# A two-model transformer kernel on one core: norm chains interleaved, retention moved forward, modulation rows turned four at a time

## The chip, the cores and the metric

The kernel runs on one core of one Trainium2 chip. The metric is the device time of one execution in microseconds (us). "PE" is TensorE, "DVE" VectorE, "ACT" ScalarE, "POOL" GpSimd, "SP" SyncE; "ACTq" in a row is a DMA issued by ScalarE. Matrices are float32 (precision is kept by splitting, see below); weights stream in from HBM, activations stay in SBUF.

## The reference, cut to what matters

```python
# first_block: DEPTH = 2, 256 latent and 256 context tokens, width 1024
for i in range(DEPTH):
    ml = split(silu(c) @ w_ada[i] + b_ada[i], 6)       # modulation, 2 streams
    mc = split(silu(c_ctx) @ w_ada[i] + b_ada[i], 6)
    u = modulate(h, g_pre_mix[i], ml[0], ml[1])        # rms_norm(h)*(1+scale)+shift
    o = even_mixer(u) if i % 2 == 0 else odd_mixer(u)  # recurrence + window | 2 attentions
    h = h + ml[2] * rms_norm(o @ w_out[i], g_post_mix[i])
    f = sqrelu_mlp(modulate(h, g_pre_ff[i], ml[3], ml[4]), w_ff1[i], w_ff2[i])
    h = h + ml[5] * rms_norm(f, g_post_ff[i])
# second block: 256 tokens, on the latent stream
p = rms_norm_2(h) @ w_in_2     # nsa q, k, v, gates | retention q, k, v, gate | 2 x 1024 gates
nsa = nsa_attention(...)       # compressed, selected and window attention
ret = retention(q, k, v)       # 4 heads; normed, times silu(gate)
z = sigmoid(ga[:, :1024]) * (nsa @ w_nsa_branch) + sigmoid(ga[:, 1024:]) * (ret @ w_ret_branch)
h = h + z @ w_mix_out; u = rms_norm_2(h); out = h + gated_mlp(u)  # with a short convolution
```

## The kernel before, in words

The whole computation is one static program. A Python function writes a **plan**, a list of steps; each engine runs through the plan and issues its own part of every step, so the order of the plan is the order of each engine's queue. Nothing is scheduled at run time: an engine blocks at its next instruction until the semaphores that it names have come.

**Weights** come in chunks of 128 x 2048 through a ring of four SBUF slots loaded by SyncE. A projection is done with split numbers: ScalarE rounds a chunk into one of three `HIGH` buffers (`split`, L2473), VectorE subtracts to leave the low part (L1906), and PE multiplies high x high, high x low and low x high in three matmuls (L1412, L1413, L1414). `early` is the place in the plan at which the next chunk's split is put: one chunk ahead. The modulation slices are not split (`whole`).

**Modulation**: 24 slices of `w_ada` per layer, two layers. `mod(i, s)` is 16 small matmuls of 128x256 (L1463) into a PSUM bank, four row groups of 32; ScalarE copies the rows (L2473, 128x256), and `turn` transposes and sums them with 4 instructions on PE (L1470) and one add on VectorE (L1899). Eight slices stand at the very front, eight in the even stage (45 to 249 us), 32 as filler in the recurrence (249 to 640 us).

**Norm chains.** Four stages end in a row projection with `gate`: mix0, ff0 (its chain is `m1`), mix1, ff1 (`m2`). For a token block of 128, "out block" takes the sum from PSUM (L1972), ScalarE squares it (L2551), VectorE gates it (L1975); `normed` then does: residual (L1961, 128x1024), square and root on ScalarE (L2514, L2516), inverse (L1931) and scale rows (VectorE L1936, half 0; ScalarE L2520, half 4), transposes on PE (L1477), out of PSUM with the modulation (VectorE L1948, ScalarE L2538), x hi (ScalarE, L2473 128x512), x lo (VectorE, L1955 128x512, two of them). mix0 and ff0 have four token blocks, mix1 and ff1 two. The next stage's projection waits for x lo. The first steps of ff1 are cut into halves of two tokens (`ff1 half`).

**Odd attention** begins with `odd start` (ScalarE issues five DMAs of tables) and qD, kD, vD. The **second block** begins with `second start` (eleven such DMAs) and qN, a projection over both token blocks. There `run(n_prepare(), r_proj())` takes the two generators in turn: the attention of the second block, and retention's q, k, its values vr, gates gr and the merge gates ga. When both have ended, `merge start` takes the sigmoid of ga (L2794, 128x4096) and the silu of gr (L2796), and the four retention heads (`ret s` L1822, `ret o` L1830, scores from PSUM L2370) run beside the projection of the nsa branch. `ret norm`, `ret gated` (L2400) and `ret turn` (PE L1844, L2407) follow alone, and then the ret branch.

## Time and profile before

| | us |
|---|---|
| median of 3 runs | 2057.84 |
| lowest, highest | 2055.41, 2064.58 |
| the profiled execution | 2063.38 |
| its span in the trace | 2061.6 |
| PE busy | 1844.8 |
| DVE busy | 1100.0 |
| ACT busy | 904.6 |
| POOL busy | 216.2 |

Busy time is from the trace. Matmuls overlap, so a group's sum can be more than the time that it fills. An idle time in brackets is that of the engine right before the row's first instruction, with what ended it.

### The profile page before, as it was taken

What the parts mean: (1) busy time and instruction counts of PE and PEld (TensorE: products, weight loads), DVE (VectorE), ACT (ScalarE), POOL (GpSimd) and SP (SyncE); (2) the same over time, 40 slices, a digit from 0 to 9 for tenths busy, and PEclk for the clock granted to TensorE, in tenths of its full rate; (3) what the DMA queues carried; (4) which work ended last, traced back from release to release, by engine and by line L of the source; (5) the groups of instructions that cost most, each with busy time, mean ns of one, the idle gap of its engine ahead of it and who ended that gap; (6) DMA issues with size and microseconds to landing.
All of it is one profiled execution on the core that took longest, in us unless ns stands there. A gap on an engine that the chain in (4) does not pass through costs nothing.

```text
span 2061.6 us, 39782 instructions
## 1 busy us (share of the span) xinstructions
PE 1844.8 (89%) x16802; PEld 1537.0 (75%) x16802; DVE 1100.0 (53%) x1671; ACT 904.6 (44%) x1448; POOL 216.2 (10%) x214
## 2 busy tenths in 40 slices
PE   5899879899888889999996999799979999679997
PEld 3777658778777778888886776698877677569985
DVE  1457565465555554324435766565445674556863
ACT  3326545344332353223325356565342465346652
POOL 0000034425253000000000200010000000000210
PEclk9999889999998989999998999899989999789998
DMA  8332233222231222333233420355544434245543
GB/s 272 94 123 90 91 112 105 85 84 84 84 105 64 82 82 82 102 102 93 91 102 72 124 81 28 107 182 187 192 131 155 152 103 139 72 132 164 184 156 110
DMA packets 201375, 237.16 MB, mean 115 GB/s; under 512 B 14347, under 2 KB 158573, under 8 KB 201197
## 3 DMA queue, kind: packets, MB, share of 16 engines
q1 hardware_dynamic: 195856, 227.33, 34.7%
q10 hardware_dynamic: 5341, 7.30, 1.0%
q8 instruction: 132, 2.16, 0.4%
q14 instruction: 46, 0.38, 0.1%
HBM read 233.56 MB, written 1.05 MB: 114 GB/s over the span
## 4 chain that ended last, share of the span: by engine, by line
PE 75%; DVE 11%; ACT 7%; issue 2%; POOL 2%; DMA 1%; SPq 1%; ACTq 1%; DVEq 0%; POOLq 0%
PE bank L1412 18%; PE bank L1413 17%; PE bank L1414 17%; PE bank L1604 9%; ACT window L2473 2%; DVE window L1906 2%; PE bank L1592 2%; PE bank L1571 2%; PE bank L1583 2%; PE bank L1463 1%; PE bank L1611 1%; SPq L2934 1%; PE bank L1789 1%; ACT arena L2538 1%; PE bank L1575 1%
## 5 line engine op out<-in xcount | busy, mean ns | idle before, releaser
L1412 PE MATMUL bank<-window 128*128 128x512 f32 (+1 forms) x2152 | 768.6, 357 | 64.8 <-DVE window L1955 27.8
L1413 PE MATMUL bank<-window 128*128 128x512 f32 (+1 forms) x2152 | 754.1, 350 | 0.0
L1414 PE MATMUL bank<-window 128*128 128x512 f32 (+1 forms) x2152 | 753.8, 350 | 0.0
L1412 PEld LDWEIGHTS bank<-window 128*128 128x128 f32 x2152 | 419.6, 195 | 131.1 <-DVE window L1906 32.4
L1906 DVE TENSOR_TENSOR window<-arena,window 128x2048 fp32r<-128x2048 f32 (+1 forms) x164 | 371.4, 2265 | 272.3 <-ACT window L2473 270.4
L2473 ACT ACTIVATE window<-arena 128x2048 fp32r<-128x2048 f32 (+3 forms) x292 | 377.1, 1291 | 198.3 <-PE bank L1414 121.4
L1414 PEld LDWEIGHTS bank<-window 128*128 128x128 f32 x2152 | 419.0, 195 | 50.9
L1413 PEld LDWEIGHTS bank<-window 128*128 128x128 f32 x2152 | 420.2, 195 | 48.1 <-issue 0.2
L2473 ACT ACTIVATE arena<-bank 128x256 f32<-128x256 f32 (+1 forms) x298 | 127.0, 426 | 370.7 <-PE bank L1414 134.9
L1604 PE MATMUL bank<-arena 64*64 64x64 f32 (+1 forms) x5888 | 218.1, 230 | 18.9 <-DVE arena L1398 10.5
L1604 PEld LDWEIGHTS bank<-arena 64*64 64x64 f32 x5888 | 204.8, 139 | 35.4 <-DVE arena L1398 12.2
L2880 POOL TENSOR_TENSOR arena<-arena 128x256 f32<-128x256 f32 x80 | 67.8, 848 | 409.1 <-ACT arena L2473 303.1
L2695 ACT ACTIVATE arena<-bank 128x512 f32<-128x512 f32 (+1 forms) x64 | 31.4, 491 | 142.0 <-PE bank L1414 140.7
L2108 DVE TENSOR_TENSOR arena<-arena,bank 128x512 f32<-128x512 f32 (+1 forms) x80 | 50.7, 634 | 64.7 <-PE bank L1604 63.7
L2597 ACT ACTIVATE arena<-bank,arena 128x512 f32<-128x512 f32 (+3 forms) x112 | 58.5, 522 | 55.0 <-DVE arena L2052 34.0
L2241 DVE TENSOR_TENSOR arena<-arena 128x512 f32<-128x512 f32 (+1 forms) x48 | 29.0, 603 | 78.8 <-ACT arena L2695 78.3
L1463 PE MATMUL bank<-arena 128*32 128x256 f32 x768 | 58.3, 426 | 13.3 <-DMA arena<-in_w_ada 13.1
L2052 DVE TENSOR_REDUCE arena<-bank 128x1 f32<-128x512 f32 (+4 forms) x96 | 51.7, 538 | 22.9 <-PE bank L1575 17.0
L2902 POOL TENSOR_TENSOR arena<-arena 128x2048 f32<-128x2048 f32 x2 | 11.1, 5560 | 483.1 <-DMA arena<-in_c_rpb 483.1
L2473 ACT ACTIVATE extra<-bank 128x512 f32<-128x512 f32 (+2 forms) x96 | 46.9, 489 | 19.4 <-PE bank L1583 16.8
L1470 PEld LDWEIGHTS bank<-arena 128*128 128x128 f32 x192 | 29.0, 213 | 25.5 <-ACT arena L2473 12.1
L1477 PE MATMUL bank<-arena 128*128 128x128 f32 x144 | 26.2, 347 | 23.8 <-DVE arena L1936 23.3
(286 smaller groups left out, 1668.1 us busy)
## 6 DMA issues: line engine op xcount, KB each, us to landing
arena<-in_w_ff SPq DMA_DIRECT2D x64, 1024.0 KB, 5.3
arena<-in_w_ada SPq DMA_DIRECT2D x48, 1024.0 KB, 5.7
arena<-in_w_in SPq DMA_DIRECT2D x23, 1024.0 KB, 5.1
arena<-in_w_ffn_up SPq DMA_DIRECT2D x22, 1024.0 KB, 5.1
arena<-in_w_ffn_down SPq DMA_DIRECT2D x10, 1024.0 KB, 5.1
arena<-in_w_in_even SPq DMA_DIRECT2D x9, 1024.0 KB, 5.5
arena<-in_w_out SPq DMA_DIRECT2D x8, 1024.0 KB, 5.1
arena<-in_w_in_odd SPq DMA_DIRECT2D x8, 1024.0 KB, 5.3
```

The costliest lines, as they stand in the source:

```text
L1412: e.matmul(o, rr(l[0]), rr(r[0]), start=start, stop=False)
L1413: e.matmul(o, rr(l[0]), rr(r[1]), start=False, stop=False)
L1414: return e.matmul(o, rr(l[1]), rr(r[0]), start=False, stop=stop)
L1463: t = e.matmul(u.b[q:q + 32, 0:256], SV[:, k, :], w.v[:, k, :], start=k < 4, stop=k >= 4)
L1571: t = e.matmul(b if it["ns"] > 1 else b[:, 0], it["q"][h0:h1], k, start=True, stop=not it["masks"])
L1604: t = e.matmul(o[h0:h1, c], l[i][h0:h1, c], r[i][h0:h1, c], start=i == 0, stop=i == len(l) - 1)
L1906: e.tensor_tensor(rr(raw), raw, rr(w.high, F32), SUB).then_inc(*ve.tick(w.ready))
L2052: e.tensor_reduce(low[:, h * ns:h * ns + ns], b, AX.X, MAX, negate=True).then_inc(*ve.tick(at("max", S, i, h)))
L2108: e.tensor_tensor(w, w, x, SUB).then_inc(*ve.tick(b.empty, at("w", *u)))
L2473: return e.activation(o, i, ACT.Copy, **k)
L2597: e.activation(a.P[i % a.NP][h][:, s * n:s * n + n], u.b[:, s * n:s * n + n], ACT.Exp, bias=low[:, x:x + 1], accum_out=total[:, x:x + 1]). ...
L2880: return e.tensor_tensor(z.L[l % 2], z.G[:, :, 0], lvl[:, 1 - d, l:l + 1, :].to_broadcast([128, NCH, 64]), MUL)
```

## The change

1. **Shared turns.** Four slices of the modulation accumulate in one PSUM bank: slice g of four shifts the two input columns by 2g rows (`SV` is 38 wide, `sel` 8). One copy of rows and one `turn` follow for each four. The bank is held over four slices.
2. **Norm chains.** The chains of token blocks are taken up at other places between the matmuls of the last out blocks; `out gate` is a step of its own; the last two chains end together (`ends`) between the first matmuls of the next stage. Scale rows is done by VectorE in both halves; x lo of half 4 is GpSimd's. `early` can hold two places: the second chunk of the next stage is split right behind the first token block's steps, its low part by GpSimd (128x2048), its high part in a fourth `HIGH` buffer, lent by `extra` outside the attentions. `ff1 half` and qD wait for both halves of two tokens' x lo.
3. **Constants.** `odd start` and `second start` come behind vD and behind the kv projections.
4. **Values first.** In the second block the first half of vr stands ahead of qN; it is a row projection of one token block at a time, and waits for that block alone.
5. **Retention.** Its heads, norm, gating and turning are a part of the first generator now and run beside the last projections of ga and the nsa branch; silu of gr comes first, the sigmoid in two halves (`gates 0`, `gates 1`). Each of the retention steps waits for what it reads. `oT` lies in H and GB.

```diff
+    turns = [0, 1, 2]
+    early = []
     chunks = {}
+    def lend(name):
+        high_free[3] = tuple(stage(name))
+        turns.insert(1, 3)
+    def back():
+        turns.remove(3)
     class Chunk:
...
+                n, w.pool = early.pop(0)
+                plan.insert(n, ("split", key))
+                early[:] = [(n + 1, q) for n, q in early]
+        if not early or whole and len(early) == 1:
+            here()
     def here():
-        early[0] = len(plan)
+        early[:] = [(len(plan), False)]
     def cols(key, W, c0, n, k0=0, nk=8, whole=False):
...
-    order_of_mod = []
+    order_of_turn = []
     def mod(i, s):
         cols(("mod", i, s), I["w_ada"][i], s * 256, 256, whole=True)
-        take("mod", i, s)
-        order_of_mod.append((i, s))
...
-        give("mod", i, s)
-    def turn_row(i, s):
-        take("turn", i, s)
-        step("turn", i, s)
-        give("turn", i, s)
+        if s % 4 == 3:
+            order_of_turn.append((i, s // 4))
+            step("rows", i, s // 4)
+            give("mod", i, s // 4)
+    def turn_rows(i, g):
+        take("turn", i, g)
+        step("turn", i, g)
...
     def modulation(i, f0=0, f1=24):
-        prev = None
         for s in range(f0, f1):
...
-                turn_row(i, prev)
-            prev = s
-            yield
-        turn_row(i, prev)
+            if s % 4 == 0 and s > f0:
+                turn_rows(i, s // 4 - 1)
+            yield
+        turn_rows(i, f1 // 4 - 1)
...
                 elif y == len(parts) - 1:
                     for m in range(ntok):
                         step("out", name, c, y - 1, (m,))
-                        if then and m > 1:
-                            next(then[m - 2])
+                        last, before = [then[i:i + 1] if i >= 0 else () for i in (m - 1, m - 2)]
+                        on_by(before, 1)
+                        on_by(last, 1)
+                        on_by(before, 2)
                         step("out", name, c, y, (m,))
-                        if then and m > 1:
-                            next(then[m - 2])
-                            next(then[m - 2])
                         step("out block", name, c, m)
+                        on_by(last, 1)
+                        if gate:
+                            step("out gate", name, c, m)
                         give("out", name, c, m)
-                        if then:
-                            last = then[m - 1] if m == ntok - 1 else iter(())
-                            next(last, None)
-                            for _ in range(3):
-                                next(then[m])
-                                next(last, None)
+                        on_by(then[m:m + 1], 1)
+                        if then and not m:
+                            early.append((len(plan), True))
             if c == 0:
                 for m in range(ntok):
                     step("out block", name, c, m)
+                    if gate:
+                        step("out gate", name, c, m)
                     give("out", name, c, m)
-        trailing[:] = then[-1:]
-        if ntok == 2:
-            trail()
+        trailing[:] = [ends(*then[-2:])] if then else []
+    def on_by(gens, n):
+        for g in gens:
+            for _ in range(n):
+                next(g)
+    def ends(a, b):
+        on_by([a, b, a, a, b], 1)
+        yield
+        on_by([b], 1)
+        yield
+        on_by([b], 2)
+        yield
     def trail(n=3):
...
+                if j == 0 and n == 256:
+                    trail()
...
                     for f in range(4):
                         take("ff1", i, 0, f)
-                    step("ff1 half", i, 0, (0, 1, 2))
+                    step("ff1 half", i, 0, (0,))
+                    trail(1)
+                    step("ff1 half", i, 0, (1, 2))
                     trail(1)
...
-            trail(2 * j - 3)
+        trail((1, 0, 1, 1)[j])
     cols(("kD",), W_o, 2048, 128)
     take("kD")
     step("kD")
...
     qN, KCV, KSW = sb(4, 256), sb(2, 2, 256), sb(2, 2, 256)
-    step("second start")
     second_x = xr
+    def values_gates(nm, j, c0, between):
+        for k in range(2):
+            take(nm, j, k)
+        for y in range(2):
+            cols((nm, j, y), W_2, c0 + j * 512, 512, y * 4, 4)
+        for k in range(2):
+            for y in range(2):
+                step("vg", nm, j, y, k)
+                if not k:
+                    between()
+            give(nm, j, k)
+    trail(1)
+    values_gates("vr", 0, 2328, lambda: trail(1))
+    trail()
     for j in range(4):
         if j % 2 == 0:
             cols(("qN", j // 2), W_2, j * 128, 256)
             take("kv", nm, g)
             step("kv", nm, g)
...
+    def retained():
+        step("end", "second attention")
+        attended.append(True)
+        step("ret start")
+        step("gates", 0)
+        spreads["ret",] = (lambda k: col("ret_gn_w_2", k), gwr, stage("second attention"))
+        yield from spread_(("ret",))
+        step("ret gates")
+        yield from staggered_(retention(h) for h in range(4))
+        step("ret norm")
+        step("gates", 1)
+        yield
+        for i in range(2):
+            step("ret gated", i)
+            yield
+            for q in (0, 4):
+                take("ret turned", i, q)
+                step("ret turn", i, q)
+                give("ret turned", i, q)
+                yield
+    def n_then_ret():
+        yield from n_prepare()
+        while len(r_turned) < 8:
+            yield
+        yield from retained()
...
-    spreads["ret",] = (lambda k: col("ret_gn_w_2", k), gwr, stage("second attention"))
-    run(spread_(("ret",)))
-    step("ret gates")
-    run(branch("nsa", I["w_nsa_branch_2"][0], 4), staggered_(retention(h) for h in range(4)))
...
+    def r_then_branch():
+        for n, _ in enumerate(r_proj()):
+            yield
+            if attended or n > 24 and n % 2:
+                yield
+        while not attended:
+            yield
+        for _ in branch("nsa", I["w_nsa_branch_2"][0], 4):
+            yield
+            yield
+    back()
+    r_turned, attended = [], []
+    run(n_then_ret(), r_then_branch())
+    step("end", "retention")
+    lend("retention")
...
+            w, u, g = chunks["mod", i, s], bank("mod", i, s // 4), s % 4
             pe.wait_ge(w.landed, u.before, at("sv"))
             for k in range(8):
                 q = 32 * (k % 4)
-                t = e.matmul(u.b[q:q + 32, 0:256], SV[:, k, :], w.v[:, k, :], start=k < 4, stop=k >= 4)
-            t.then_inc(*pe.tick(u.full, w.used))
...
-            e.tensor_scalar(scaled_rows(k, 0), rows_of(k, 0), RS[:, k, 2:3], None, MUL).then_inc(*ve.tick(at("scaled rows", T, k, 0)))
+            for q in (0, 4):
+                e.tensor_scalar(scaled_rows(k, q), rows_of(k, q), RS[:, k, 2:3], None, MUL).then_inc(*ve.tick(at("scaled rows", T, k, q)))
         def norm_x(T, k, q):
...
+        def ret_start():
             sc.wait_ge(sc.last(), *stage("second attention"))
             load(landed_decay, at("decay"), [(dec, C["dec"])])
             copy(rr(oNh), oN).then_inc(*sc.tick(at("oN rounded")))
-            sc.wait_ge(sc.last())
-            e.activation(ga, ga, ACT.Sigmoid).then_inc(*sc.tick(at("gates")))
-            sc.wait_ge(sc.last())
+            sc.wait_ge(sc.last(), *[at("vg", "gr", j, 1) for j in range(2)])
             e.activation(gr, gr, ACT.Silu).then_inc(*sc.tick(at("gr")))
+        def gates(i):
+            g = ga[:, :, 1024 * i:1024 * i + 1024]
+            sc.wait_ge(sc.last(), *[at("vg", "ga", 2 * i + j, 1) for j in range(2)])
+            e.activation(g, g, ACT.Sigmoid).then_inc(*sc.tick(at("gates", i)))
...
+        def split(key):
+            w = chunks[key]
+            if w.pool:
+                raw = w.ap[:, 0:w.n]
+                gp.wait_ge(gp.last(), w.rounded)
+                e.tensor_tensor(rr(raw), raw, rr(w.high, F32), SUB).then_inc(*gp.tick(w.ready))
         def part_o(k):
...
```

VectorE at the end of ff0, third and fourth token block, before (L1961 residual, L1936 scale rows, L1948 out of PSUM, L1955 x lo, L1972 and L1975 the last out block):

```order
L1975 TENSOR_TENSOR arena<-arena 128x512 [waits scalar_done,vector_done]
L1931 RECIPROCAL arena<-arena 128x1 [waits scalar_done,vector_done]
L1961 SCALAR_TENSOR_TENSOR arena<-arena 128x1024 [waits vector_done]
L1931 RECIPROCAL arena<-arena 128x1 [waits scalar_done,vector_done]
L1936 TENSOR_SCALAR arena<-arena 128x4x128 [waits vector_done]
L1948 TENSOR_SCALAR arena<-bank,arena 128x128 [waits tensor_done,vector_done]
L1948 TENSOR_SCALAR arena<-bank,arena 128x128 [waits vector_done] x3
L1955 TENSOR_TENSOR window<-arena,window 128x4x128 [waits scalar_done,vector_done] x2
L1969 TENSOR_SCALAR arena<-arena 128x1 [waits vector_done]
L1972 TENSOR_TENSOR arena<-arena,bank 128x512 [waits tensor_done,vector_done]
L1975 TENSOR_TENSOR arena<-arena 128x512 [waits scalar_done,vector_done]
L1948 TENSOR_SCALAR arena<-bank,arena 128x128 [waits tensor_done,vector_done]
```

The same stretch with the change (L2052 residual, L2026 scale rows, L2038 out of PSUM, L2046 x lo, L2063 and L2072 the out block):

```order
L2052 SCALAR_TENSOR_TENSOR arena<-arena 128x1024 [waits pool_done,vector_done]
L2060 TENSOR_SCALAR arena<-arena 128x1 [waits vector_done]
L2063 TENSOR_TENSOR arena<-arena,bank 128x512 [waits tensor_done,vector_done]
L2020 RECIPROCAL arena<-arena 128x1 [waits scalar_done,vector_done]
L2026 TENSOR_SCALAR arena<-arena 128x4x128 [waits vector_done]
L2026 TENSOR_SCALAR arena<-arena 128x4x128
L2072 TENSOR_TENSOR arena<-arena 128x512 [waits scalar_done,vector_done]
L2020 RECIPROCAL arena<-arena 128x1 [waits scalar_done,vector_done]
L2052 SCALAR_TENSOR_TENSOR arena<-arena 128x1024 [waits vector_done]
L2038 TENSOR_SCALAR arena<-bank,arena 128x128 [waits tensor_done,vector_done]
L2038 TENSOR_SCALAR arena<-bank,arena 128x128 [waits vector_done] x3
L2046 TENSOR_TENSOR window<-arena,window 128x4x128 [waits scalar_done,vector_done]
```

Scale rows is two instructions on VectorE, x lo one, and the fourth block's residual (L2052) stands ahead of the third block's transposed rows.

GpSimd with the change, from the end of the recurrence's last step to the third tail (L2988 the low part of a chunk, L2981 x lo, L3005 the bias of the odd attention); before, it holds none of L2988 and L2981:

```order
L2994 TENSOR_TENSOR window<-arena,window 128x512 [waits pool_done]
L2988 TENSOR_TENSOR window<-arena,window_extra 128x2048 [waits scalar_done,pool_done]
L2981 TENSOR_TENSOR window<-arena,window 128x4x128 [waits scalar_done,pool_done] x4
L2988 TENSOR_TENSOR window<-arena,window_extra 128x2048 [waits scalar_done,pool_done]
L2981 TENSOR_TENSOR window<-arena,window 128x4x128 [waits scalar_done,pool_done] x4
L3005 TENSOR_TENSOR arena<-arena 128x2048 [waits landed_bias,landed_odd,pool_done]
L3005 TENSOR_TENSOR arena<-arena 128x2048 [waits pool_done]
L2988 TENSOR_TENSOR window<-arena,window_extra 128x2048 [waits scalar_done,pool_done]
L2981 TENSOR_TENSOR window<-arena,window 128x4x128 [waits scalar_done,pool_done] x2
```

GpSimd's low part of 128x2048 stands right ahead of the x lo steps of the same tail.

ScalarE where retention starts, before (L2794 sigmoid, L2796 silu, L2801 and L2807 the heads, L2473 copies and splits):

```order
L2487 DMA arena<-t_dec 128x1536 [waits vector_done,tensor_done,scalar_done]
L2473 ACTIVATE window<-arena 128x1024
L2794 ACT_TABLE_LOAD
L2794 ACTIVATE arena<-arena 128x4096 [waits scalar_done]
L2796 ACT_TABLE_LOAD
L2796 ACTIVATE arena<-arena 128x2048 [waits scalar_done]
L2473 ACTIVATE arena<-bank 128x512 [waits tensor_done,scalar_done]
L2473 ACTIVATE window<-arena 128x2048 [waits landed_ring1,scalar_done]
L2801 ACTIVATE arena<-bank 128x256 [waits tensor_done,scalar_done]
L2473 ACTIVATE window<-arena 128x2048 [waits landed_ring2,scalar_done]
L2801 ACTIVATE arena<-bank 128x256 [waits tensor_done,scalar_done]
L2807 ACTIVATE extra,arena<-arena 128x256 [waits vector_done,scalar_done]
```

With the change (L2881 silu, L2886 sigmoid of a half, L2891 and L2897 the heads, L2564 copies and splits):

```order
L2564 ACTIVATE arena<-bank 128x512 [waits tensor_done,scalar_done]
L2578 DMA arena<-t_dec 128x1536 [waits pool_done,vector_done,scalar_done]
L2564 ACTIVATE window<-arena 128x1024
L2881 ACT_TABLE_LOAD
L2881 ACTIVATE arena<-arena 128x2048 [waits scalar_done]
L2886 ACT_TABLE_LOAD
L2886 ACTIVATE arena<-arena 128x2x1024 [waits scalar_done]
L2564 ACTIVATE arena<-bank 128x512 [waits tensor_done,scalar_done]
L2891 ACTIVATE arena<-bank 128x256 [waits tensor_done,scalar_done]
L2564 ACTIVATE window<-arena 128x2048 [waits landed_ring3,scalar_done]
L2891 ACTIVATE arena<-bank 128x256 [waits tensor_done,scalar_done]
L2897 ACTIVATE extra,arena<-arena 128x256 [waits vector_done,scalar_done]
```

The silu is first, the sigmoid is 2048 wide instead of 4096, and a copy of a ga bank (L2564, 128x512) stands between it and the heads.

## Rows read from the trace of the kernel before

**Rows 1.** The page's first part: busy time, share, instructions by engine.

```profile
PE 1844.8 (89%) x16802; PEld 1537.0 (75%) x16802; DVE 1100.0 (53%) x1671; ACT 904.6 (44%) x1448; POOL 216.2 (10%) x214
```

**Rows 2.** The page's chain that ended last, by engine.

```profile
PE 75%; DVE 11%; ACT 7%; issue 2%; POOL 2%; DMA 1%; SPq 1%; ACTq 1%; DVEq 0%; POOLq 0%
```

**Rows 3.** Waits of PE: engine, line, released by: us, times, longest.

```profile
PE bank L1412 <- DVE window L1955: 27.8, 8, 5.5
PE bank L1412 <- DVE window L1906: 27.4, 10, 7.9
```

**Rows 4.** Windows: length, busy time by engine, granted clock (1.00 is 2.4 GHz), DMA.

```profile
249.00:640.00 391.00, 344.38 (x8074) 296.22 (x8075) 212.24 (x393) 164.43 (x327) 153.15 (x154) 0.93 0.30 97
1740.00:1790.00 50.00, 30.33 (x117) 24.39 (x116) 24.04 (x42) 28.73 (x48) 6.64 (x2) 0.74 0.22 79
```

**Rows 5.** Timeline, PE, five tails: start, us, instruction, [idle before <-releaser].

```profile
745.16 0.58 PE L1412 MATMUL bank<-window 128*128 128x256 f32 x1 [3.93 <-DVE window L1906]
...
1103.62 1.97 PE L1477 MATMUL bank<-arena 128*128 128x128 f32 x8 [5.42 <-DVE arena L1936]
...
1123.82 0.58 PE L1412 MATMUL bank<-window 128*128 128x256 f32 x1 [7.89 <-DVE window L1906]
...
1135.19 0.51 PE L1412 MATMUL bank<-window 128*128 128x512 f32 x1 [2.04 <-DVE window L1955]
...
1310.01 1.97 PE L1477 MATMUL bank<-arena 128*128 128x128 f32 x8 [6.37 <-DVE arena L1936]
1316.24 0.58 PE L1412 MATMUL bank<-window 128*128 128x256 f32 x1 [4.26 <-DVE window L1955]
...
1507.20 1.97 PE L1477 MATMUL bank<-arena 128*128 128x128 f32 x8 [6.13 <-DVE arena L1936]
1513.07 0.58 PE L1412 MATMUL bank<-window 128*128 128x256 f32 x1 [3.90 <-DVE window L1955]
```

**Rows 6.** Timeline, ScalarE and then VectorE, behind the second and fourth tails.

```profile
1119.46 1.91 ACT L2473 ACTIVATE window<-arena 128x2048 fp32r<-128x2048 f32 x1 [2.99 <-issue]
...
1518.83 5.80 ACT L2473 ACTIVATE window<-arena 128x2048 fp32r<-128x2048 f32 x3 [6.67 <-issue]
...
1121.48 2.29 DVE L1906 TENSOR_TENSOR window<-arena,window 128x2048 fp32r<-128x2048 f32 x1 [5.30 <-ACT window L2473]
```

**Rows 7.** GpSimd's line L2902 by itself, then VectorE's timeline beside it.

```profile
L2902 POOL TENSOR_TENSOR arena<-arena x2: 4579/5560/6542, 1150.0 to 1154.6; 128x2048 f32<-128x2048 f32 x2
...
1150.72 5.98 DVE L1906 TENSOR_TENSOR window<-arena,window 128x2048 fp32r<-128x2048 f32 x1 [0.35 <-ACT window L2473]
```

**Rows 8.** Timeline, VectorE, third tail.

```profile
1302.01 0.49 DVE L1936 TENSOR_SCALAR arena<-arena 128x512 f32<-128x512 f32 x1
...
1314.77 1.42 DVE L1955 TENSOR_TENSOR window<-arena,window 128x512 fp32r<-128x512 f32 x2 [1.78 <-ACT window L2473]
```

**Rows 9.** GpSimd's groups by form: busy us, mean ns, idle before.

```profile
L2891 POOL TENSOR_TENSOR window<-arena,window 128x512 fp32r<-128x512 f32 x7 | 8.9, 1265 | 0.6
```

**Rows 10.** Timeline of the retention stage, ScalarE and then PE.

```profile
1742.45 3.62 ACT L2794 ACTIVATE arena<-arena 128x4096 f32<-128x4096 f32 x1
...
1755.94 1.22 PE L1830 MATMUL bank<-arena 128*128 128x256 f32 x2 [4.74 <-DVE arena L2370]
...
1778.40 1.94 PE L1844 MATMUL bank<-arena 128*128 128x128 f32 x8 [7.89 <-DVE arena L2400]
1783.96 1.97 PE L1844 MATMUL bank<-arena 128*128 128x128 f32 x8 [3.62 <-DVE arena L2400]
```

**Rows 11.** Windows of L1470 alone; ScalarE's group of copies; chain of 249:640 by line.

```profile
45.00:249.00 204.00, 6.05 (x36) 5.28 (x36) 0.97 0.31 95
249.00:640.00 391.00, 18.69 (x128) 17.25 (x128) 0.93 0.30 97
...
L2473 ACT ACTIVATE arena<-bank 128x256 f32<-128x256 f32 x238 | 91.2, 383 | 215.6 <-PE bank L1604 80.7 <-PE bank L1611 64.1 <-PE bank L1463 42.7
...
by line: PE bank L1604 46.6%; PE bank L1463 4.9%; PE bank L1611 4.8%; issue 3.0%; PE bank L1470 2.5%; DVE arena L2141 2.0%; PE bank L1687 1.9%; DVE arena L2108 1.8%; DVE arena L2218 1.5%; POOL arena L2880 1.4%; DVE arena L2149 1.4%; PE bank
```

189 lines of the change are left out of this document (97 added, 92 removed).

## The prediction

> **What bounds the kernel.** The parts of the page come first. PE is busy for 1844.8 us of 2061.6 [rows 1], and the chain that ended last lies on PE for 75%, on DVE for 11% and on ACT for 7% [rows 2]. So the time is PE's work plus what PE waits for, and a change that leaves its matmuls as they are can win only in the waits and in the small instructions between. The list of PE's waits comes next: 27.8 us for x lo (L1955) and 27.4 us for the low part of a weight chunk (L1906) [rows 3]. Both stand where one stage hands over to the next. The timeline of PE shows them one by one [rows 5]; the windows show where the clock falls with them: 0.74 of full in the retention stage, where PE is busy for 30.33 us of 50 [rows 4].
>
> **The tails, summed wait by wait.** The profiled execution took 2063.4 us; the terms are differences to it.
>
> *mix0 (four blocks).* The 3.93 us wait for L1906 [rows 5] is for the second chunk of ff1, whose split stands behind all the chains. Now ScalarE rounds it behind the first block's steps and GpSimd subtracts, long before it is wanted. It goes: **-4**. Some 4 us more of waits for the last blocks' chains could go if nothing new is late: -7.9 is the best end, 0 the worst.
>
> *ff0 (four blocks).* Same chunk, larger wait: 7.89 us [rows 5], because ScalarE's split waits behind its five table DMAs (2.99 us idle), takes 1.91, and L1906 takes 2.29 [rows 6]. The split moves ahead and the DMAs move behind vD; 7.89 goes. Of the waits that are the chain itself, 5.42, 2.47 and 2.04 [rows 5], squares that no longer stand behind matmul-bound steps take some 2 off, the rest is late as before: **-10**, ends -12.6 and -6.
>
> *mix1 (two blocks).* Here the waits, 6.37 and 4.26 [rows 5], are the last block's chain alone, and no chunk is late, so there is nothing for the early split to give. There is something for it to take: GpSimd's subtraction of 128x2048 takes at least 4.58 us [rows 7]. With the rounding right behind the first block's gate it would run at about 1300 to 1304.7, over the moment at which VectorE scales the first block's rows (1302.01) [rows 8]. What that costs turns on contention. The trace has the pair once: a L1906 that began 0.8 us into GpSimd's 128x2048 took 5.98 us in place of 2.29 [rows 6, 7], that is, it waited until GpSimd was done (3.7 us) and then ran. If scale rows is held in the same way it ends 2.7 us later, and the last block's chain with it. To that come the second half of scale rows, now on VectorE (0.49) [rows 8], and x lo of half 4 on GpSimd, 1.27 us [rows 9] in place of 0.71, half of a row's 1.42 [rows 8]: 2.7 + 0.49 + 0.56 = **+4** (rounded up from 3.8). Without contention it is 0.49 + 0.56, +1; if the squares' and residual's order adds a second hit, +6.
>
> The row shows a two-input subtraction held; scale rows has one input, so the row does not settle it. The Trainium skill (SBUF — State Buffer, Who interferes with whom) says that a `tensor_scalar` in a two-port mode takes the port pair that it shares with GpSimd, and that whichever starts first keeps it for its whole instruction. Here the 128x512 form took 0.49 us where the two-input form took 0.71 [rows 8], so it does run at a faster rate, which by that page means that it is held. By the page mix1 is at +4, by a reading in which only two-input forms are held it is at +1. I take the first, for the rate in the row.
>
> *ff1 (two blocks).* 6.13 and 3.90 [rows 5]. The values of the second block now come first, one token block at a time, so PE has matmuls of block 0 while the last chain runs: the 3.90 goes. The same 0.49 + 0.56 comes to the chain and some contention: **-2.5**, ends -4.6 and +1.
>
> The eleven table DMAs (6.67 us of ScalarE) [rows 6] leave this place too. They come back behind kv, where PE has queued matmuls to cover them; if the first rotations wait for them it costs up to 3: **+0.5**. The norm in front of the gated MLP and the very first one take the longer x lo and second scale rows without any gain: **+1.5** together (0.49 + 0.56 each, and a little). The attention rounds of the second block lose the first half of vr as filler. The nearest row of a round without filler is the 4.74 us wait [rows 10]: ends 0 and +4.7, **+1.5** taken, since six filler steps in seven stay.
>
> Tails and these: -4 - 10 + 4 - 2.5 + 0.5 + 1.5 + 1.5 = **-9**.
>
> **Retention.** In the window of 50 us PE stands idle for 19.7 [rows 4]. Three waits make 16.25 of it: 4.74 for the first scores, behind which lies the sigmoid of 128x4096 (3.62 us) ahead of all else on ScalarE, and 7.89 and 3.62 for L2400, when nothing is left beside `ret gated` and `ret turn` [rows 10]. With the change all three have ga's last projections or the nsa branch beside them. The matmuls are the same, only their place changes. **-16**. Ends: -22, if all the idle time goes and the clock stays up over half of the stretch; -10, if the filler runs out ahead of the second turn and half of the 11.5 stays. What is new on ScalarE's queue is `gates 1` (half of 3.62 and a table load) between the heads and the turns; the nsa half of the gates is done before.
>
> **Turns.** 36 of 48 turns go, with 36 row copies (0.383 us each on ScalarE) [rows 11]. In the even stage 36 L1470 instructions take 6.05 us, so 24 fewer are 4.0; some of that PE time lies beside waits: **-3.3**. In the recurrence 128 take 18.69 us [rows 11]; 96 fewer are 14.0. The chain there has 2.5% of 391 us on L1470, 9.8 us for 128, so 7.3 for 96 [rows 11]; the copies and adds that the recurrence's own small steps queue behind add something. Between 7.3 and 14.0, **-10**; ends -14 and 0. In the front stretch the slices wait for their weights, nothing changes.
>
> **Sum.** -9 - 16 - 3.3 - 10 = -38.3. On the profiled 2063.4 that is 2025.1. The median of the runs is 5.5 lower, 2057.8; less 38.3 it is 2019.5, so **2020 us**.
>
> **Rivals.**
> *B, no contention.* GpSimd and VectorE don't hold each other, and what the chains no longer wait for goes: tails -7.9 - 12.6 + 1 - 4.6 = -24.1 in place of -12.5, 12 us better: **2008**. For it: the chains' order is better in all four. Against it: the 5.98 us row.
> *C, gains off the path.* PE waits in the recurrence for other steps of the chain (46.6% of it is L1604, the rest spread over DVE and POOL) [rows 11], so shorter turns give 0 in place of 10; retention gives 10 in place of 16: -22.3, **2035**.
> *D, handover waits come back one step later.* The worst ends of the tails (0 - 6 + 6 + 1 = +1), 3.5 for the rest, retention -10, even stage -3.3, recurrence 0: -8.8, **2049**. For it: every tail's last chain is as long as before or longer, and qD and the halves of ff1 wait for both halves of x lo.
> *E, slower.* A group of four slices holds one of the eight PSUM banks throughout the recurrence, so seven rotate for its steps. ScalarE empties 238 banks in the 128x256 form, 0.383 us each [rows 11]. If PE had to wait for one more such copy at each use, that would be 91 us: 91 - 38 = +53, **2111**. It decides from 38.3 / 238 = 0.16 us a use. Against it: PE is busy for 344.4 of 391 us there, DVE for 212 and ACT for 164 [rows 4], so banks are emptied quickly and 47 us of idle time have other causes; and 48 short uses for slices and turns fall away.
>
> **Chances.** Forecast (A) 0.45 (its own range 2009 to 2031), B 0.17, C 0.22, D 0.08, E 0.08. 0.5%, about what a measurement of this kernel can tell from no change, is 10.3 us, so faster means under 2047.5. A, B and C lie there but for 0.02 of C: 0.82. D and that rest make 0.10 within 0.5%, E 0.08 slower. The range reaches from B's lower part (its 2008 less the recurrence's 4 and retention's 6, 1998, and 2 for rounding) to D: 1996 to 2048 leaves out E, most of D and a little of B, under 0.2.
>
> **What would show it.** Right: no wait for a chunk's low part in the mix0 and ff0 tails; a wait of 6 to 10 us at the ff1 of mix1 and scale rows of over 2 us beside GpSimd's 128x2048; in the retention stage no PE wait over 3 us and a clock over 0.85; L1470's successor x48; the recurrence's window 7 to 14 us shorter. Wrong: scale rows at 0.49 us beside GpSimd (B); the recurrence as long as before (C); new waits of PE for banks in it (E); the retention stage with long waits for L2400's successor still there (D).

## The result, and the profile after

The changed kernel takes 2044.99 us (median of 6 runs, 2040.02 to 2049.54), the kernel before 2061.51 us in the same comparison (6 runs, 2055.41 to 2064.58). The ratio is 0.9922, 95% interval 0.9907 to 0.9937: 16.5 us or 0.8% faster. Forecast were 38 us. The profiled execution took 2046.16 us with a span of 2044.3, 17.3 us less than the span before.

The page of the changed kernel: span, busy time, and the chain that ended last by engine (before: [rows 1, 2]).

```profile
span 2044.3 us, 39320 instructions
...
PE 1821.5 (89%) x16658; PEld 1505.3 (74%) x16658; DVE 1100.9 (54%) x1631; ACT 881.3 (43%) x1397; POOL 254.9 (12%) x236
...
PE 74%; DVE 10%; ACT 8%; POOL 3%; issue 2%; DMA 2%; ACTq 1%; SPq 0%; DVEq 0%; POOLq 0%
```

PE is busy as large a share of a shorter span. POOL's part of the chain has grown from 2% to 3%. The list of PE's waits says where, with the columns of [rows 3]:

```profile
PE bank L1499 <- POOL window L2981: 40.0, 9, 7.3
...
PE bank L1499 <- DVE window L1995: 17.5, 10, 4.0
```

The waits for the low part of a chunk (L1906 before, now L1995) went from 27.4 to 17.5 us. In the place of 27.8 us for x lo on VectorE there are 40.0 us for x lo on GpSimd (L2981). The timeline of PE in the four tails, as in [rows 5]; two rows each for mix0, ff0 and ff1, three for mix1:

```profile
724.13 0.58 PE L1499 MATMUL bank<-window 128*128 128x256 f32 x1 [3.57 <-POOL window L2981]
...
743.43 0.38 PE L1499 MATMUL bank<-window 128*128 128x256 f32 x1 [1.99 <-POOL window L2981]
...
1095.66 0.58 PE L1499 MATMUL bank<-window 128*128 128x256 f32 x1 [3.57 <-POOL window L2981]
...
1114.52 0.47 PE L1499 MATMUL bank<-window 128*128 128x512 f32 x1 [2.86 <-POOL window L2981]
...
1288.14 1.09 PE L1564 MATMUL bank<-arena 128*128 128x128 f32 x8 [2.63 <-DVE arena L2026]
...
1295.85 1.97 PE L1564 MATMUL bank<-arena 128*128 128x128 f32 x8 [6.62 <-DVE arena L2026]
1302.62 0.58 PE L1499 MATMUL bank<-window 128*128 128x256 f32 x1 [4.81 <-POOL window L2981]
...
1496.47 0.76 PE L1499 MATMUL bank<-window 128*128 128x512 f32 x1 [6.05 <-POOL window L2981]
...
1509.11 0.76 PE L1499 MATMUL bank<-window 128*128 128x512 f32 x1 [3.56 <-POOL window L2981]
```

The 3.93 and 7.89 us waits for a late chunk are gone. Of the rest, those of the two short tails are within 0.4 us of what they were or longer (6.37 and 4.26 became 6.62 and 4.81; 6.13 and 3.90 became 6.05 and 3.56), and in seven of the nine rows PE waits for GpSimd. In both short tails a wait is new: PE waits 2.63 us in mix1, and 2.67 in ff1 (at 1489.33), for the scale rows of the first of the two blocks. Before, the transposes of that block (L1477 at 1302.55) began without a wait.

**Stage by stage.** The start of one and the same instruction in both traces gives the lag of the changed kernel; its change over a stage is what the stage gave or took. The forecast's term stands beside it.

| stage | measured, us | forecast |
|---|---|---|
| front and even stage, to 250 | -0.2 | -3.3 |
| recurrence, 250 to 660 | -7.5 | -10 |
| mix0 and its tail, 660 to 765 | -3.2 | -4 |
| ff0's projections, 765 to 1075 | +2.3 | 0 |
| ff0's tail, 1075 to 1145 | -12.1 | -10 |
| behind it, 1145 to 1175 | +3.5 | 0 |
| mix1's tail, 1280 to 1325 | +3.6 | +4 |
| ff1's tail, 1490 to 1530 | +0.8 | -2.5 |
| behind it, 1530 to 1585 | +1.4 | +0.5 |
| attention and retention, 1585 to 1800 | -9.2 | -14.5 |
| norm ahead of the gated MLP | +2.1 | +1 |
| the rest | +1.2 | +0.5 |
| sum | -17.3 | -38.3 |

In ff1's tail 48 matmuls of the values are moved in, 0.227 us apart, 11 us; they are taken off there (the lag itself goes from -13.3 to -1.5) and added to the attention.

One trace's lag is good to some 3 us in a stage with clock changes: in the 12 traces with shared turns, which have the same code up to 640 us, the lag there is -3.4 to -9.7 us, mean -8.1. Where two traces have the same waits and the granted clock differs, the difference is not told as an effect below.

### The profile page after: what moved, and what is told of

Read it like the earlier page. It is cut to its first block, busy times and chain, and to the rows that moved or that the text cites. A ratio compares the mean times of both kernels' runs of the same rounds, so it can differ in the third digit from the quotient of the medians.

```text
span 2044.3 us, 39320 instructions
## 1 busy us (share of the span) xinstructions
PE 1821.5 (89%) x16658; PEld 1505.3 (74%) x16658; DVE 1100.9 (54%) x1631; ACT 881.3 (43%) x1397; POOL 254.9 (12%) x236
## 4 chain that ended last, share of the span: by engine, by line
PE 74%; DVE 10%; ACT 8%; POOL 3%; issue 2%; DMA 2%; ACTq 1%; SPq 0%; DVEq 0%; POOLq 0%
PE bank L1499 17%; PE bank L1501 17%; PE bank L1500 17%; PE bank L1691 9%; ACT window L2564 2%; DVE window L1995 2%; PE bank L1679 2%; PE bank L1658 2%; DMA arena<-in_w_ada 2%; PE bank L1670 1%; PE bank L1550 1%; ACT arena L2625 1%; PE bank L1698 1%; PE bank L1876 1%; PE bank L1564 1%
## 5 line engine op out<-in xcount | busy, mean ns | idle before, releaser
L1501 PE MATMUL bank<-window 128*128 128x512 f32 (+1 forms) x1988 | 687.2, 346 | 0.0
L1499 PE MATMUL bank<-window 128*128 128x512 f32 (+1 forms) x1716 | 620.0, 361 | 57.8 <-POOL window L2981 40.0
L1500 PE MATMUL bank<-window 128*128 128x512 f32 (+1 forms) x1880 | 670.9, 357 | 0.0
L1499 PEld LDWEIGHTS bank<-window 128*128 128x128 f32 x1716 | 334.1, 195 | 115.0 <-issue 35.1
L1501 PEld LDWEIGHTS bank<-window 128*128 128x128 f32 x1988 | 385.0, 194 | 45.2
L1500 PEld LDWEIGHTS bank<-window 128*128 128x128 f32 x1880 | 366.0, 195 | 47.7 <-issue 0.5
L1995 DVE TENSOR_TENSOR window<-arena,window 128x2048 fp32r<-128x2048 f32 (+1 forms) x132 | 297.4, 2253 | 190.3 <-ACT window L2564 188.7
L2564 ACT ACTIVATE window<-arena 128x2048 fp32r<-128x2048 f32 (+3 forms) x260 | 316.7, 1218 | 168.4 <-DMA arena<-in_w_ff 51.1
L2564 ACT ACTIVATE arena<-bank 128x256 f32<-128x256 f32 (+1 forms) x262 | 113.5, 433 | 365.8 <-PE bank L1501 132.1
L2988 POOL TENSOR_TENSOR window<-arena,window_extra 128x2048 fp32r<-128x2048 f32 x4 | 18.4, 4601 | 598.4 <-ACT window_extra L2564 598.4
L1995 DVE TENSOR_TENSOR window<-arena,window_extra 128x2048 fp32r<-128x2048 f32 (+1 forms) x28 | 63.1, 2255 | 46.8 <-ACT window_extra L2564 46.7
L1499 PE MATMUL bank<-window,window_extra 128*128 128x256 f32 (+1 forms) x272 | 82.3, 303 | 0.0
L1500 PE MATMUL bank<-window,window_extra 128*128 128x256 f32 (+1 forms) x272 | 81.8, 301 | 0.0
L1499 PE MATMUL bank<-window_extra,window 128*128 128x512 f32 x164 | 66.5, 405 | 4.6 <-DVE window L1995 4.5
```

Source lines behind the costliest of these rows:

```text
L1499: e.matmul(o, rr(l[0]), rr(r[0]), start=start, stop=False)
L1500: e.matmul(o, rr(l[0]), rr(r[1]), start=False, stop=False)
L1501: return e.matmul(o, rr(l[1]), rr(r[0]), start=False, stop=stop)
L1995: e.tensor_tensor(rr(raw), raw, rr(w.high, F32), SUB).then_inc(*ve.tick(w.ready))
L2564: return e.activation(o, i, ACT.Copy, **k)
```

## The experiments

All ratios are against the kernel before on the same chip. E1 to E4 share one set of runs of it (median 2061.4), E5 to E8 another (2061.9), E9 to E11 a third (2063.7).

**E1, shared turns alone.** The kernel before with part 1 of the change.

```diff
-                t = e.matmul(u.b[q:q + 32, 0:256], SV[:, k, :], w.v[:, k, :], start=k < 4, stop=k >= 4)
+                t = e.matmul(u.b[q:q + 32, 0:256], SV[:, k, 6 - 2 * g:38 - 2 * g], w.v[:, k, :], start=g == 0 and k < 4, stop=g == 3 and k >= 4)
```

> Before with the shared turns alone: four slices accumulate in a bank, one row copy and one turn for each four. Theory (what the two traces' difference suggests): a turn costs PE its issue distance of about 0.42 us (4 instructions), not the 0.6 us that the busy time gives; the recurrence gains 7 to 8 us and the even stage 0.2 to 2, in all 8 to 10 us, 2052 against 2061. Rival: the recurrence's gain in the changed kernel came from somewhere else, and this kernel gains under 4 us. Rival E of the prediction (a held bank costs waits): slower than before.

Measured: 2053.9 us, 0.9958 (0.9941 to 0.9975): 7.5 us faster by the medians, 8.7 by the ratio. So about half of the whole gain is this part, and the held bank costs nothing that shows. The windows of the turn's line in the changed kernel (before: [rows 11]):

```profile
45.00:249.00 204.00, 2.25 (x12) 1.97 (x12) 0.97 0.31 95
249.00:640.00 391.00, 4.69 (x32) 4.33 (x32) 0.93 0.30 97
```

The busy time falls by 3.8 and 14.0 us, the time by less: matmuls overlap, and a turn's four instructions move PE on by 0.42 us (the lag steps by that, once for each turn that goes), not by 0.58 (18.69 / 32) as the busy time has it. 24 turns give 10 us at most in the recurrence; the mean over the 12 traces is 7.3. In the even stage the lag also steps down by 0.42 each time, and comes up again by 0.3 to 0.7 a little later (at 160, 182, 205, 228 and 244 us), where PE stands idle that much longer.

**E2, the early chunk's low part on VectorE; E3, x lo on VectorE; E4, both.** The kernel after, at the same places of the plan.

```diff
-                            early.append((len(plan), True))
+                            early.append((len(plan), False))
```

```diff
-            if not q:
-                lo, hi = [a[:, 0:4, k * 128:k * 128 + 128] for a in (X.lo, X.hi)]
+            lo, hi = [a[:, q:q + 4, k * 128:k * 128 + 128] for a in (X.lo, X.hi)]
```

> The changed kernel, with the low part of the early chunk on VectorE in place of GpSimd, at the same place of the plan. Theory (contention): scale rows beside it take 0.49 us again in place of 3.1, VectorE is held for 2.3 us instead of 2.6, so the two short tails (mix1, ff1) gain 0 to 1 us each and the long ones stay within 1 us. If GpSimd's help was real help, the tails get slower by up to 2.3 us each, 9 in all.

> The changed kernel, with x lo of half 4 on VectorE again (0.69 us in place of 1.27). Theory: GpSimd's x lo starts only once VectorE's own x lo is through and holds the next scale rows (1.32 us in place of 0.49), so PE's waits for x lo get 0.6 to 1.4 us shorter at each of its 9 places: 6 to 10 us faster in all. Rival: the halves run side by side anyway, difference under 2 us.

> The changed kernel with both of these on VectorE: no GpSimd in the norm chains. Theory (contention is the lost part of the tails): 8 to 12 us faster than the changed kernel, of which mix1 gives 3 to 4, ff1 3, the long tails 1 to 2 each. If contention costs little and VectorE's queue is the bound, no better than the changed kernel or slower.

Measured: 2036.6 us, 0.9884 (0.9857 to 0.9912); 2034.4 us, 0.9865 (0.9842 to 0.9887); 2030.5 us, 0.9849 (0.9823 to 0.9876). The changed kernel's interval begins at 0.9907. Those of E3 and E4 lie below it, so both are faster than the changed kernel; that of E2 reaches 0.9912, so its 8.4 us by the medians are likely and not shown by the total alone. Without GpSimd the gain over the kernel before nearly doubles: 31 us in place of 16.5. So GpSimd's part in these chains was no help, though on VectorE's queue its steps take 2.3 us for each early chunk and 0.7 for each x lo. The two edits don't add: 8.4 and 10.6 us alone, 14.5 together.

What happens is to be seen in the third tail of the changed kernel: VectorE, then GpSimd; and VectorE's scale rows over the whole execution (minimum/median/maximum in ns).

```profile
1284.99 3.49 DVE L2026 TENSOR_SCALAR arena<-arena 128x512 f32<-128x512 f32 x2
...
1294.47 1.71 DVE L2026 TENSOR_SCALAR arena<-arena 128x512 f32<-128x512 f32 x2
...
1283.23 4.57 POOL L2988 TENSOR_TENSOR window<-arena,window_extra 128x2048 fp32r<-128x2048 f32 x1 [135.71 <-ACT window_extra L2564]
1294.25 1.26 POOL L2981 TENSOR_TENSOR window<-arena,window 128x512 fp32r<-128x512 f32 x1 [6.45 <-ACT window L2564]
```

```profile
L2026 DVE TENSOR_SCALAR arena<-arena x36: 473/484/3186, 31.6 to 1826.3; 128x512 f32<-128x512 f32 x36
```

Scale rows takes 0.48 us by itself. The first one begins 1.8 us into GpSimd's 4.57 and takes 3.10 us: it ends 0.28 us behind GpSimd (3.49 is for the two). This is what PE's new wait of 2.63 us is for. The first of the second pair begins 0.2 us into x lo, takes 1.32 us (1.71 for the two), and again ends 0.28 us behind GpSimd. The same tail in E2, where x lo is still GpSimd's (VectorE, GpSimd, PE):

```profile
1276.41 2.29 DVE L1995 TENSOR_TENSOR window<-arena,window_extra 128x2048 fp32r<-128x2048 f32 x1
...
1279.12 0.88 DVE L2026 TENSOR_SCALAR arena<-arena 128x512 f32<-128x512 f32 x2
...
1285.99 1.72 DVE L2026 TENSOR_SCALAR arena<-arena 128x512 f32<-128x512 f32 x2
...
1285.76 1.27 POOL L2981 TENSOR_TENSOR window<-arena,window 128x512 fp32r<-128x512 f32 x1 [145.69 <-ACT window L2564]
...
1279.66 1.09 PE L1564 MATMUL bank<-arena 128*128 128x128 f32 x8 [0.97 <-DVE arena L2026]
```

The split takes 2.29 us on VectorE and the first pair of scale rows 0.88; the second pair still has 1.72, beside the x lo. PE's new wait falls from 2.63 to 0.97. By the lag, mix1's tail is +3.6 us in the changed kernel, +2.5 in E2, +2.7 in E3 and +0.8 in E4, in which the waits are 0.97, 6.50 and 4.26. So GpSimd's two steps are 2.8 of the 3.6 us, where the prediction had 2.7 + 0.56 for them. E2's expectation missed at the long tails, which were to stay within 1 us: mix0's gives 6.2 us in place of 3.2, ff0's 14.6 in place of 12.1.

Here the one-input `tensor_scalar` is held as the two-input subtraction was in [rows 7], so the rule of the Trainium skill (SBUF — State Buffer, Who interferes with whom) that was weighed in the prediction is borne out: 3.10 us in place of 0.48. VectorE's reads from PSUM beside GpSimd are not stretched (the 128x128 form of L2038 0.41 us beside it and alone), as that page has it for an instruction with at most one input in SBUF, outside such a mode.

**E5, another order of the last two chains.** On E4: scale rows of the last block ahead of x lo of the one before, and the last transposes ahead of the first values.

```diff
-        on_by([a, b, a, a, b], 1)
+        on_by([a, b, a, b, a], 1)
...
-    trail(1)
+    trail(2)
     values_gates("vr", 0, 2328, lambda: trail(1))
```

> The kernel of e4 (no GpSimd in the norm chains), with the last two chains in another order: scale rows of the last block ahead of x lo of the block before it, and in the second block the last block's transposes ahead of the first values. Theory (queue order is what is left in the two short tails): the last scale rows waits for two x lo, 1.4 us, and their x hi; 2 us off the wait of mix1 (6.5), 3 to 4 us off the ff1 tail, 0 to 2 in the long ones: 2025 against 2030. Rival (the chain's own length is the bound): under 1 us.

Measured: 2027.7 us, 0.9832 (0.9807 to 0.9856): by the medians 3 us better than E4, which is inside the intervals, so the total does not show it. The tails do. PE's waits in mix1 and ff1 in E4, then in E5:

```profile
1286.24 1.97 PE L1564 MATMUL bank<-arena 128*128 128x128 f32 x8 [6.50 <-DVE arena L2026]
1292.47 0.58 PE L1499 MATMUL bank<-window 128*128 128x256 f32 x1 [4.26 <-DVE window L2045]
...
1484.12 0.77 PE L1499 MATMUL bank<-window 128*128 128x512 f32 x1 [5.50 <-DVE window L2045]
...
1495.17 0.47 PE L1499 MATMUL bank<-window 128*128 128x512 f32 x1 [3.02 <-DVE window L2045]
```

```profile
1289.28 1.97 PE L1564 MATMUL bank<-arena 128*128 128x128 f32 x8 [4.38 <-DVE arena L2026]
1295.51 0.58 PE L1499 MATMUL bank<-window 128*128 128x256 f32 x1 [4.26 <-DVE window L2045]
...
1486.24 1.97 PE L1564 MATMUL bank<-arena 128*128 128x128 f32 x8 [4.01 <-DVE arena L2026]
```

6.50 has become 4.38, and of 5.50 and 3.02 one wait of 4.01 is left. The lag gets 1.2 us better in mix1 and 3.0 in ff1. So the queue's order was a part of what the prediction called the chain itself. No run here shortens what remains (4.38 and 4.26).

**E6, the fourth high buffer for the early chunk alone, and the constants elsewhere.** On E4.

```diff
-                i = turns.pop(0)
-                turns.append(i)
+                i = 3 if early and early[0][1] else turns.pop(0)
+                if i < 3:
+                    turns.append(i)
...
+    step("odd start")
     cols(("kD",), W_o, 2048, 128)
...
-    step("odd start")
     back()
...
+        if nm == "kcv":
+            step("second start")
```

> The kernel of e4, with two edits in separate stages. First, the fourth high buffer takes the early chunk alone and doesn't rotate with the other three: theory, matmuls that read it are issued 2 to 9 ns further apart, so the projections of ff0 (765 to 1075 us) get the 2.4 us back that every kernel with the rotating fourth buffer lost there; rival, the 2.4 us come from something else and stay. Second, the odd stage's table DMAs stand ahead of kD and the second block's between its two key projections, where ScalarE is idle: theory 2 to 3 us off the 3.5 that are given back behind the ff0 tail and 1 us at 1530; rival, that loss is GpSimd's mask bias, which begins with the tables and would only move: 0.

Measured: 2023.9 us, 0.9814 (0.979 to 0.9839); by the medians 6.5 better than E4, the intervals overlap. In ff0's projections the lag rises by 2.3 to 2.6 us in all traces with the rotating buffer, by 0.0 in E1 and by 0.2 here. Groups of the changed kernel in that stretch (busy us, mean ns of one):

```profile
L1500 PE MATMUL bank<-window 128*128 128x512 f32 x390 | 152.1, 390 | 0.0
...
L1499 PE MATMUL bank<-window_extra,window 128*128 128x512 f32 x56 | 22.3, 399 | 0.3 <-DVE window L1995 0.3
...
L1499 PE MATMUL bank<-window,window_extra 128*128 128x512 f32 x48 | 19.1, 398 | 0.0
L1500 PE MATMUL bank<-window,window_extra 128*128 128x512 f32 x48 | 18.8, 392 | 0.0
```

A matmul that reads `window_extra` takes 392 to 399 ns where the others take 389 to 390, and those that read it are the ones issued further apart. Their larger distances add up to 1.3 of the 2.3 us; the other 1.0 is spread thinly over the rest of the stage, and goes in E6 as well. What the rotation does there is not shown.

The constants' part holds too: from 1145 to 1175 the lag rises by 1.5 us in place of 3.1, from 1530 to 1585 by 0.0 in place of 1.4. But the trace of E6 loses 2.8 us between 1175 and 1280, where E4's loses nothing: the same two waits (0.81 and 1.76 us) are followed by a granted clock of 0.50 from 1247 to 1254 in E6, and of 1.00 in E4. Three of the four traces with the constants at their new places have this loss (2.8 us, in E9 2.9, in E11 1.6, in E10 none), and none of the other eight has it. Whether it belongs to the edit is open.

What is left behind ff0's tail is another contention. E4, VectorE and then GpSimd with the mask bias, which waits for those constants:

```profile
1134.52 6.01 DVE L2382 SCALAR_TENSOR_TENSOR arena<-arena 128x512 f32<-128x512 f32 x3
...
1130.14 9.59 POOL L3004 TENSOR_TENSOR arena<-arena 128x2048 f32<-128x2048 f32 x2 [472.06 <-DMA arena<-t_flip]
```

Of the three L2382 in those 6.01 us one takes 4.67; the line's median is 0.49. In E6 the three take 6.19.

**E7, retention's gates on VectorE and an early root; E8, also both gatings ahead of the turns.** E7 on E4, E8 on E7. In E7 the step `ret gates` is VectorE's (twice 128x1024), no longer GpSimd's.

```diff
-        step("ret gates")
         yield from staggered_(retention(h) for h in range(4))
+        step("ret gates")
...
+    step("root table")
     for c in range(2):
         for m in range(2):
             take("mix2", c, m)
```

```diff
         for i in range(2):
             step("ret gated", i)
-            yield
+        yield
+        for i in range(2):
             for q in (0, 4):
```

> The kernel of e4, with the retention gates' product with the norm weights on VectorE behind the heads in place of GpSimd beside them, and a dummy root ahead of the last projection. Theory: PE's 4.8 us wait for the second scores is VectorE's split held by GpSimd (4.38 us for 2.29, and 1.85 for 0.35 ahead of it), so it shrinks by 3 to 4; what VectorE does instead costs 0 to 1 behind; the table load of 1.28 us in front of the gated MLP's norm goes. 4 to 5 us in all. Rival: the wait stays, since the split stood ahead of the scores in the queue anyway: 1.3 us in all.

> The kernel of e7, with both gating steps of retention in one piece ahead of the turns. Theory: PE's 6.5 us wait at the third turn is the second gating, which stands on VectorE behind a chunk's split, two products of the nsa branch and the first turns' low parts; it goes all but 1 us, the first turn comes 2 us later: 4 us better than e7. Rival: the wait moves to the first turn or to the branch, no gain.

Measured: 2019.4 us, 0.9803 (0.9779 to 0.9826), and 2019.2 us, 0.98 (0.976 to 0.984). E7 is 11 us better than E4 by the medians (the intervals touch), where 4 to 5 were expected. Its own stages account for 6.1 (3.2 in retention and 2.9 at the norm); up to there its trace is 3.6 ahead with the same code. E8's runs lie from 2012 to 2029, so the total tells nothing about its edit; its trace is 4.9 us better in retention. First the changed kernel: PE's two waits, then VectorE and GpSimd ahead of the first of them, then ScalarE and VectorE ahead of the second.

```profile
1731.73 1.22 PE L1917 MATMUL bank<-arena 128*128 128x256 f32 x2 [4.80 <-DVE arena L2461]
...
1760.69 1.09 PE L1931 MATMUL bank<-arena 128*128 128x128 f32 x4 [6.48 <-DVE arena L2491]
...
1724.81 1.85 DVE L2468 TENSOR_SCALAR arena<-arena 128x256 f32<-128x256 f32 x1
1726.70 4.38 DVE L1995 TENSOR_TENSOR window<-arena,window 128x2048 fp32r<-128x2048 f32 x1
...
1724.14 4.79 POOL L3011 TENSOR_TENSOR arena<-arena 128x1024 f32<-128x1024 f32 x2 [215.18 <-ACT arena L2564]
...
1749.31 1.91 ACT L2886 ACTIVATE arena<-arena 128x2048 f32<-128x2048 f32 x1
...
1753.27 2.29 DVE L1995 TENSOR_TENSOR window<-arena,window 128x2048 fp32r<-128x2048 f32 x1 [3.02 <-ACT window L2564]
```

The waits that the prediction let go [rows 10] are gone at their own places and have come back at a later step. The 4.74 was for the first head's scores; the 4.80 is for the third's, which the expectation of E7 calls the second. The 7.89 was for the first gating, and its turn (1750.40) now begins without a wait; the second gating, for which PE had waited 3.62, it now waits 6.48 for. The 4.80 comes about like this: VectorE's step on these scores (L2461) stands behind a chunk's low part that took 4.38 us in place of 2.29, behind a 1.85 that should be 0.35, both beside GpSimd's product. In E7 (VectorE, then PE):

```profile
1704.63 2.29 DVE L1996 TENSOR_TENSOR window<-arena,window 128x2048 fp32r<-128x2048 f32 x1 [1.40 <-ACT window L2569]
1706.96 0.56 DVE L2461 TENSOR_TENSOR arena<-bank,arena 128x384 f32<-128x384 f32 x1
...
1707.57 0.70 PE L1918 MATMUL bank<-arena 128*128 128x256 f32 x2 [2.46 <-DVE arena L2461]
...
1727.74 1.06 PE L1932 MATMUL bank<-arena 128*128 128x128 f32 x8 [2.64 <-DVE arena L2496]
...
1736.16 1.09 PE L1932 MATMUL bank<-arena 128*128 128x128 f32 x4 [3.03 <-DVE arena L2496]
```

The low part takes 2.29 and the wait is 2.46. At the turns 2.64 and 3.03 remain; in E8:

```profile
1728.72 1.06 PE L1933 MATMUL bank<-arena 128*128 128x128 f32 x8 [2.65 <-DVE arena L2497]
...
1739.71 0.50 PE L1501 MATMUL bank<-window 128*128 128x512 f32 x1 [0.84 <-DVE window L1997]
```

So the 6.48 us was VectorE's queue: the second gating stood behind a chunk's split, two products of the nsa branch and the first turns' low parts. Filler on PE does not help there, since the filler's own VectorE steps stand ahead of what PE waits for. That queue also began late: VectorE stood idle for 3.02 us ahead of that split, because ScalarE's part of it stood behind `gates 1`, a table load of 1.28 and the sigmoid of 1.91 us. No run moves `gates 1` by itself. And the row of ScalarE in the changed kernel that has no counterpart before:

```profile
1822.47 1.28 ACT L2607 ACT_TABLE_LOAD   x1
```

The sigmoid of the second half of the gates now comes behind `ret norm`, so the root's table has to be loaded again at the gated MLP's norm, on the chain. E7 gets that stage from E4's +1.9 to -1.0 us. That is more than the load: the granted clock in E4's trace is low twice there (0.54 from 1804 to 1811 and 0.53 from 1815 to 1822), in E7's once (0.51 from 1804 to 1811).

**E9, all of these edits together.**

> All edits together: the changed kernel with no GpSimd in the norm chains, the last chains' new order, the fourth high buffer for the early chunk alone, both table loads of constants in ScalarE's idle stretches, and both retention edits with the early root. If the stages are independent, 2019 of e8 less 3 to 4.6 (chains' order), 2.4 (fourth buffer) and 1.6 to 3 (constants): 2009 to 2012. Rival: the steps that each stage gives are given back by the clock in the next: over 2016.

Measured: 2005.4 us (5 runs, 2001.55 to 2008.7), 0.972 (0.97 to 0.9739). That beats both kernels: 58 us under the kernel before. Expected were 2009 to 2012.

**E10, on E9, GpSimd's mask bias in pieces of 128x512.**

```diff
-                e.tensor_tensor(bias[:, qt, :, :], bias[:, qt, :, :], cmask...[128, 8, 256], ADD)
+                for h in range(0, 8, 2):
+                    e.tensor_tensor(bias[:, qt, h:h + 2, :], bias[:, qt, h:h + 2, :], cmask...[128, 2, 256], ADD)
```

> The kernel of e9, with GpSimd's mask bias in eight instructions of 128x512 in place of two of 128x2048. Theory (whoever begins holds the other for its whole instruction): the longest VectorE instruction beside it falls from 4.7 us to under 2, in all VectorE is held a third or less as long, PE's wait behind it gets 1 us shorter: 0 to 2 us better. Rival (they share at a reduced rate): VectorE's instructions beside it are stretched in sum as before.

Measured: 2009.6 us (2000.7 to 2013.1), 0.9734 (0.971 to 0.9759): no difference in the total. VectorE, then GpSimd:

```profile
1125.29 4.64 DVE L2385 SCALAR_TENSOR_TENSOR arena<-arena 128x512 f32<-128x512 f32 x3
1129.96 3.25 DVE L1998 TENSOR_TENSOR window<-arena,window 128x2048 fp32r<-128x2048 f32 x1
...
1121.48 12.87 POOL L3013 TENSOR_TENSOR arena<-arena 128x512 f32<-128x512 f32 x8 [463.77 <-DMA arena<-in_c_rpb]
```

Three of L2385, 7.04 us for them in E9, take 4.64; the chunk's low part, 2.29 in E9 because GpSimd was through by then, takes 3.25. VectorE is held 1.4 us less, a quarter and not the two thirds expected, and GpSimd takes 12.87 in place of 9.56. Shorter pieces shorten each hold (the longest L2385 takes 1.79 us) and share it out. PE's waits behind it are 2.32 and 1.00 us in E9 and one of 1.96 here, and the lag between 1145 and 1175 rises by 0.9 in place of 2.4 us. The total is too coarse to show it.

**E11, on E9, the first values behind the first queries.**

```diff
-    trail(2)
-    values_gates("vr", 0, 2328, lambda: trail(1))
     trail()
...
         give("qN", j)
+    values_gates("vr", 0, 2328, lambda: None)
```

> The kernel of e9, with the first values behind the second block's first queries in place of ahead of them, and the queries waiting for both token blocks as before. Theory (values first covers part of the last chain): PE waits 4 to 7 us longer at the ff1 tail. Rival (what it covers is lost to the order of the transposes and to the clock): within 1 us.

Measured: 2011.3 us (2007.8 to 2014.3), 0.975 (0.9731 to 0.9769), 6 us slower than E9 by the medians; the intervals touch. PE in that tail:

```profile
1473.34 1.97 PE L1566 MATMUL bank<-arena 128*128 128x128 f32 x8 [4.01 <-DVE arena L2028]
1479.21 0.58 PE L1501 MATMUL bank<-window 128*128 128x256 f32 x1 [3.90 <-DVE window L2047]
```

The 3.90 of [rows 5] is back; over the tail the lag is 4.0 us worse. So values first is worth 4 us, as soon as the order of the transposes lets it.

## Why the prediction was wrong

The direction and the range held (2045 in 1996 to 2048), the size did not: 16.5 us measured, 38 forecast. The four tails by themselves came out nearly as forecast, -10.9 us for -12.5. Of the 21 us that the trace falls short of the forecast, the turns are 5.6, attention and retention 5.3, the constants 4.4, ff1's tail 3.3 and the fourth buffer 2.3. By its steps:

- **The late chunks in mix0 and ff0** (3.93 and 7.89): right, both waits are gone and the two tails give 3.2 and 12.1 us.
- **mix1, +4**: right, +3.6, by the two steps of GpSimd that it named (2.8 of it by E4). The place was another: the held scale rows did not lengthen the wait for the last block's chain (6.37 became 6.62) but made a new one of 2.63 us for the first block's.
- **ff1, -2.5**: wrong, +0.8. The step that failed is "PE has matmuls of block 0 while the last chain runs". It has them, but the last block's transposes stand behind 12 of them in PE's queue, and its scale rows stands behind x lo on VectorE, beside GpSimd (E4, E5: -4.4 and -7.4). The wait of 2.67 us for the first block's scale rows is new here too.
- **x lo on GpSimd, 0.56 us a piece**: mis-sized. It begins when VectorE's own x lo ends and then holds the next scale rows by 0.8 us; E3 gives 10.6 us for it by the medians, over 9 places where PE waits.
- **Constants, +0.5**: mis-sized, 3.5 and 1.4 behind the two tails; E6 gives 1.6 and 1.4 of it back. The prediction found cover for them on PE but did not ask what GpSimd's mask bias, which waits for them, would then collide with.
- **Retention, -16**: the step that failed is "all three have the projections or the branch beside them". The three waits of 16.25 us in all became 4.80 and 6.48, each at a later step of the same kind. PE had filler; what it waited for was VectorE, held by GpSimd once (E7) and queued behind the filler's own steps once (E8). `gates 1`, which the prediction named on ScalarE's queue and gave no price, is a part of the second. The sign named for a right forecast, no wait over 3 us, did not come; the granted clock did rise, to 0.86 (1718 to 1768 us) from 0.74.
- **The sigmoid moved behind the root**: missing. It costs a table load of 1.28 us on the chain.
- **Turns, -13.3**: mis-sized, 7.7 in the trace, 7.5 to 8.7 alone (E1). The term took busy time where the distance between instructions counts (10 us at most in the recurrence), and counted the even stage's share as a gain where PE only stands idle that much longer a little later.
- **The fourth buffer**: missing, +2.3 us.
- **Two readings** did no harm to the sum: L1604, taken for other steps of the recurrence's chain, is a matmul of PE itself, and the 238 copies are those of the whole execution (214 of them lie between 249 and 640 us). The 2.47 of the ff0 tail stands in the trace (at 1108.06) but not in [rows 5].
- **Rivals.** B (no contention) is refuted for this kernel. E4 comes close to what it describes: its four tails sum to -25.4, where B has -24.1; it takes 2030 and not 2008 because the other terms were too large. D (2049) comes nearest in the total, and its mechanism, handover waits that come back later, is what retention shows; but its tails (+1) and its recurrence (0) are not what was measured. C's recurrence (0) did not come about, nor did E.
